# All ten tiles of the final residual addition on TensorE instead of seven, in a hybrid-attention and MoE layer

## The reference, cut to what matters

```
x   = x + gate2 * y
out = x * rsqrt(mean(x * x) + eps) * final_norm_g
```

## Time and profile before

| what | us |
|---|---|
| median of 3 runs | 1615.78 (1613.52 to 1616.71) |
| time of the profiled execution | 1616.98 |
| its span, first to last instruction | 1615.2 |
| TensorE's last matmul group starts | 1599.57 |
| VectorE's last instruction starts | 1610.77 |

### The profile page before, as it was taken

The page is one execution under the profiler, slowest core; times in us unless marked ns, Lnnn a source line. Parts: engine busy times, 40 slices in busy tenths (PEclk is TensorE's granted clock), DMA queues, the critical chain, the costliest instruction groups (busy, mean ns, idle before and its releaser), DMA issues.

```text
span 1615.2 us, 22297 instructions
## 1 busy us (share of the span) xinstructions
PE 1528.0 (95%) x8284; PEld 1275.9 (79%) x8284; DVE 973.8 (60%) x1466; ACT 665.1 (41%) x899; POOL 306.0 (19%) x231
## 2 busy tenths in 40 slices
PE   4999999999999989999999999999999699999966
PEld 3688888888888768888788887888888588888852
DVE  5388534045536477778777763334457777777737
ACT  6522221221122466666555632111221376676643
POOL 1021111122215201001100000000000155565520
PEclk9899999999999999999999999999999599999998
DMA  9236344230001010002200024425203379999966
GB/s 369 77 150 210 148 162 153 106 113 26 26 30 63 9 67 1 0 0 89 97 0 0 33 98 155 140 88 191 84 40 144 119 220 269 275 268 267 275 132 260
DMA packets 52876, 199.98 MB, mean 124 GB/s; under 512 B 8522, under 2 KB 17594, under 8 KB 41424
## 3 DMA queue, kind: packets, MB, share of 16 engines
q1 hardware_dynamic: 42576, 173.89, 29.7%
q0 software_dynamic: 10240, 25.28, 7.9%
HBM read 157.03 MB, written 45.15 MB: 125 GB/s over the span
## 4 chain that ended last, share of the span: by engine, by line
PE 41%; DVE 9%; DMA 6%; ACT 4%; issue 3%; POOL 1%; DVEq 0%; POOLq 0%; SPq 0%; ACTq 0%
PE psum L1594 7%; DMA xg<-h2d,x_row 4%; PE psum L1550 4%; PE psum L1695 4%; PE psum L1767 4%; PE psum L1788 4%; PE psum L1536 2%; PE psum L1533 2%; PE psum L1534 2%; PE psum L1771 2%; PE psum L1519 2%; PE psum L1704 2%; PE psum L1521 2%; PE psum L1520 2%; ACT prob L1875 2%
## 5 line engine op out<-in xcount | busy, mean ns | idle before, releaser
L352 PE MATMUL psum<-h_hi,w_hi 128*128 128x512 f32 x720 | 182.6, 362 | 2.1 <-issue 2.1
L352 PE MATMUL psum<-h_lo,w_hi 128*128 128x512 f32 x720 | 179.8, 358 | 0.0
L352 PE MATMUL psum<-h_hi,w_lo 128*128 128x512 f32 x720 | 179.4, 357 | 0.0
L2112 DVE TENSOR_TENSOR pT_lo<-psum,pT_hi 128x512 fp32r<-128x512 f32 x192 | 126.3, 686 | 55.2 <-ACT pT_hi L1881 55.2
L689 POOL TENSOR_TENSOR w_lo<-w_raw,w_hi 128x1024 fp32r<-128x1024 f32 x32 | 79.2, 2475 | 337.9 <-ACT w_hi L539 337.9
L1881 ACT CAST pT_hi<-psum 128x512 fp32r<-128x512 f32 x192 | 104.5, 588 | 84.2 <-PE psum L1550 84.0
L352 PEld LDWEIGHTS psum<-h_hi,w_hi 128*128 128x128 f32 x720 | 119.7, 188 | 23.8 <-issue 3.5
L352 PEld LDWEIGHTS psum<-h_lo,w_hi 128*128 128x128 f32 x720 | 119.5, 188 | 21.7 <-issue 0.5
L352 PEld LDWEIGHTS psum<-h_hi,w_lo 128*128 128x128 f32 x720 | 119.5, 188 | 21.2
L833 DVE SCALAR_TENSOR_TENSOR ada_junk<-adaT,cs_rows 128x1024 f32<-128x1024 f32 x64 | 85.9, 1342 | 69.5 <-DMA adaT<-in_w_adaT 66.6
L1875 ACT ACTIVATE prob<-psum,nmax,q_row 128x1536 f32<-128x1536 f32 x64 | 104.6, 1634 | 32.1 <-DVE nmax L2106 32.0
(11 more groups left out here) (374 smaller groups left out, 3056.6 us busy)
## 6 DMA issues: line engine op xcount, KB each, us to landing
gu_raw<-in_w_gu SPq DMA_DIRECT2D x32, 1024.0 KB, 5.8
w_raw<-in_w_in SPq DMA_DIRECT2D x16, 1024.0 KB, 4.8
adaT<-in_w_adaT SPq DMA_DIRECT2D x16, 1024.0 KB, 6.0
dn_raw<-in_w_dn SPq DMA_DIRECT2D x16, 1024.0 KB
gates<-gst SPq DMA_DIRECT2D x14, 640.0 KB, 3.1
y_sum<-stage SPq DMA_DIRECT2D x13, 512.0 KB, 5.0
xt<-in_x SPq DMA_DIRECT2D x10, 512.0 KB, 7.7
merged<-gates SPq DMA_DIRECT2D x8, 640.0 KB, 3.9
```

Of the source, the lines that this page charges most:

```text
L352: mm = pe.matmul(psum[:, par_sets[j] + g:par_sets[j] + g + w], a[j][:, k, :], b[:, k, g:g + w], start=(k == 0 and a is w_hi and b is h_hi) ...
L2112: nc.vector.tensor_tensor(pT_lo[b][g % 2][:], psum[:, TP + 512 * b:TP + 512 * b + 512], pT_hi[b][g % 2][:], ALU.subtract).then_inc(s[f"a_t ...
```

## The change

The list of tiles that VectorE adds is gone. TensorE forms the sum of all ten tiles in PSUM, in the order 0 to 9, with tile t in slot t modulo 4; from tile 4 on, residual t waits until VectorE has finished tile t-4. ScalarE waits for TensorE's `f_sum` for every tile. VectorE's `join`, the semaphore `f_summed` and the three calls are taken out; its order is otherwise the same.

```diff
--- before.py
+++ after.py
@@ -1245,16 +1245,14 @@
                 body()
 
         y = [at(f"y_{t}", [P, D], F32, RKV + 4 * t * KB) for t in range(TILES)]
-        BY_PE = (0, 1, 2, 3, 4, 6, 8)
-        BY_DVE = [t for t in range(TILES) if t not in BY_PE]
 
         def total(t):
 
-            return psum[:, 1024 * (BY_PE.index(t) % 4):1024 * (BY_PE.index(t) % 4) + D] if t in BY_PE else x1[:, t, :]
+            return psum[:, 1024 * (t % 4):1024 * (t % 4) + D]
 
         final_g = at("final_g", [P, D], F32, RA + 24 * KB)
         junk = [at(f"junk{j}", [P, D], F32, RA + (28 + 4 * j) * KB) for j in range(2)]
-        for n in "clear gated sum summed sq rt normed st dve_c".split():
+        for n in "clear gated sum sq rt normed st dve_c".split():
             s["f_" + n] = sem("b6_" + n)
         with nc.Block() as block:
             @block.sync
@@ -1842,9 +1840,8 @@
                 if_spare(pe, body)
 
                 def residual(t):
-                    n = BY_PE.index(t)
-                    if n >= 4:
-                        pe.wait_ge(s["f_normed"], BY_PE[n - 4] + 1)
+                    if t >= 4:
+                        pe.wait_ge(s["f_normed"], t - 3)
                     for h in (0, 512):
                         pe.matmul(total(t)[:, h:h + 512], ident[:], x1[:, t, h:h + 512], start=True, stop=False)
 
@@ -1856,12 +1853,12 @@
                 pe.wait_ge(s["e_y"], 2 * NE)
                 pe.wait_ge(s["f_clear"], 1)
                 pe.wait_ge(s["f_all"], 1)
-                for t in BY_PE[0:4]:
+                for t in range(4):
                     residual(t)
-                for n, t in enumerate(BY_PE):
+                for t in range(TILES):
                     join(t)
-                    if 3 <= n < len(BY_PE) - 1:
-                        residual(BY_PE[n + 1])
+                    if 3 <= t < TILES - 1:
+                        residual(t + 1)
 
             @block.scalar
             def _(act):
@@ -2080,10 +2077,7 @@
                 nc.scalar.activation(rt[:, 0:1], eps[:], ACT.Sqrt)
 
                 for t in range(TILES):
-                    if t in BY_PE:
-                        act.wait_ge(s["f_sum"], BY_PE.index(t) + 1)
-                    else:
-                        act.wait_ge(s["f_summed"], BY_DVE.index(t) + 1)
+                    act.wait_ge(s["f_sum"], t + 1)
                     nc.scalar.activation(junk[t % 2][:], total(t), ACT.Square, accum_out=ssq[:, t:t + 1]).then_inc(s["f_sq"], 1)
                     act.wait_ge(s["f_sq"], t + 1)
                     if t % 2:
@@ -2524,10 +2518,6 @@
                     dve.wait_ge(landed[t], Y_IN[t])
                     tt(y[t][:], y[t][:], gt2_row[int(t >= CTX_TILES)][:].rearrange("p k n -> p (k n)"), ALU.mult).then_inc(s["f_gated"], 1)
 
-                def join(t):
-                    dve.wait_ge(s["f_gated"], t + 1)
-                    tt(x1[:, t, :], x1[:, t, :], y[t][:], ALU.add).then_inc(s["f_summed"], 1)
-
                 def finish(t):
 
                     r, a, b = rstd[:, t:t + 2], nsq[:, t:t + 2], ntmp[:, t:t + 2]
@@ -2544,9 +2534,6 @@
                 for t in range(0, TILES, 2):
                     gate(t)
                     gate(t + 1)
-                    for u in (t, t + 1):
-                        if u in BY_DVE:
-                            join(u)
                     if t == 4:
                         dve.wait_ge(s["f_final"], 16)
                     if t >= 4:
```

## The result

Over eleven runs each the changed kernel takes 1619.31 us (1618.70 to 1621.11) and the kernel before 1614.38 us (1611.96 to 1617.00): ratio 1.003 with a 95% interval of 1.0021 to 1.0039, slower by 3.4 to 6.3 us. The forecast was 1619.8 us and +4.0. The medians lie 4.93 us apart.

A forecast was written before the change was run, and what follows sets the result against it. VectorE ran longest, with TensorE also near its limit. VectorE's 2.28 us freed against waits of 2.80 and 3.52 us for TensorE's added tiles gave +4.04 us, taking the median 1615.78 to 1619.8 us; range 1617.5 to 1621.9.

The forecast's parts named there:

- Part 1: VectorE's additions go: tile 5's is hidden already, those of tiles 7 and 9 free 2 x 1.14 = 2.28 us.
- Part 2: TensorE gets three tiles more, 10.3 us; twelve groups 1.72 us apart from residual 4 at 1590.34, ending at 1611.24.
- Part 3: TensorE's added waits for VectorE's PSUM slots and gates are met in advance: 0, at most 1.2 us; tightest margin 1.3 us.
- Part 4: After tile 9's y pass: square 0.04, root 1.43, reciprocal 0.11, last pair 3.26 us; VectorE ends at 1616.08.
- Part 5: Stores at the end: none added or dropped, so the last 3.16 us stay.
- The sum: End of VectorE moves from 1612.04 to 1616.08, +4.04 us; median becomes 1619.8 us, slower by 0.25%.
- Rival A: Added TensorE passes overlap, VectorE stays the bound and loses two additions: 1613.5 us, 0.14% down; chance 0.06.
- The rule from the Trainium skill: Judge TensorE's headroom by weight loads' busy share: over half its time free, three tiles hidden; the prediction held against it.
- Rival B: Mechanism holds, but an earlier clock rise in TensorE's first stretch keeps the difference under 3.2 us: about 1618.7 us; chance 0.20.
- Rival C: Clock falls back inside the tail, 2 us per 4 us at half clock: 1621.8 us or far more; chance 0.04.

The follow-up runs named there:

- the first experiment: Changed kernel, but tile 5's addition stays on VectorE while tiles 7 and 9 move to TensorE; ratio to the kernel before 0.9994 (0.9984 to 1.0005).
- the dead additions: Changed kernel with three VectorE additions put back as dead work into a buffer nothing reads; ratio to the kernel before 1.0018 (1.0006 to 1.0031).
- early residuals: First four residuals made without the wait for `f_all`, behind four idle copies; ratio to the kernel before 0.9982 in that kernel, 1.0000 in the changed one.
- late residuals: Residual passes of tiles 4 to 9, removed from the changed kernel with their PSUM slot waits kept; ratio to the kernel before 0.9992 (0.9980 to 1.0005).

## Why the prediction was right

*Part 1, the additions.* The addition of tile 5 was hidden: shown by the first experiment, where it costs nothing on VectorE and 3.44 us on TensorE. Those of tiles 7 and 9 were on the path, but mis-sized: I took 1.14 us for one from the distance of two starts, and the removal gave 1.25 to 1.28. In the kernel before, gates 6 and 7 began at 1591.39, 3.53 us ahead of the step at 1594.92; in the changed one it is 1591.88 - 1589.62 = 2.26. With it VectorE alone would have gained 2.5 instead of 2.28 us. It did not matter to the end, because TensorE sets it.

*Part 2, TensorE's twelve groups.* Predicted 20.90 us from residual 4 to the end of y 9 (1590.34 to 1611.24); measured 1588.56 to 1607.55 + 1.88, 20.87. This was the term that made the sum.

*Part 3, the waits at nothing.* Right: no group behind the first starts late. That the nearest wait was met 1.3 us in advance was right as well (tile 2's pass ended at 1592.87 + 1.28 = 1594.15, and residual 6 started at 1595.53: 1.38); the dead additions used up that margin, and only then did the residuals of tiles 6 and 8 come late.

*Part 4, the last step.* Predicted 0.04, 1.43, 0.11 and 3.26 us; measured from the end of y 9 at 1609.43: 0.10, 1.43, 0.11 and 3.27. The 0.06 us is nearly all that was off here.

*Part 5, the stores.* 1617.5 - 1614.34 = 3.16 us, as before.

*The sum.* +4.04 predicted, +4.08 in F. The medians differ by 4.93, with 3.4 to 6.3 in the interval; 0.3 us of the excess shows in this trace as a later rise of the clock, and the rest can't be told from the scatter of the tail's start. That the median of 1619.31 us lies only 0.5 us from the forecast is in part luck: the kernel before came out 1.4 us lower over eleven runs than over the three on which the forecast stood, and the difference 0.9 us larger, and the two nearly cancel. The dead additions, whose tail is within 0.3 us of the changed kernel's, measured 1.0018 in another batch, which is another sign of how wide that scatter is.

*Rival A* (VectorE stays the bound) is out: it needed some 2.0 us of TensorE per tile by the prediction, and each tile took 3.44. (Worked out again from the same rows: for tile 9's square to be in time as well, all six tiles could cost at most 2.2 us each. The finish that the prediction calls the third, of tiles 6 and 7, is the fourth.) It is true of the kernel with one tile moved. The rule from the Trainium skill (Perfetto Trace Analysis, Identifying the Most-Contended Engine) spoke for it: weight loads were busy 1.74 to 1.85 of 4 us while TensorE had no gap and held everybody up. Here the measurement decides against the weight loads' share as a sign of free time; the share of peak arithmetic, which that section names beside it, was not worked out.

*Rival B* (difference under 3.2 us by an earlier rise of the clock) did not come about: the interval is 3.4 to 6.3 us, and in the profiled executions the first sixteen records took 8.76 us in the kernel before and 8.81 to 9.98 in the others that ran them behind the wait, later and never sooner. Its mechanism is real all the same: in the pair of kernels with early residuals, where the first y passes run at the full clock, the kernel before could use only 1.25 us of TensorE's gain, since the addition of tile 5 stood in the way, and the difference in G was 2.83 us.

*Rival C* (the clock falls back) did not happen in the changed kernel, granted 1.00 to the end of its passes. It did in the kernel without late residuals, so the mechanism is real in this tail; but it needs a TensorE that idles, and the change left it none.

## What to carry to other kernels

Before moving work to another engine, lay out that engine's starts in the stage in question and extend them by what it gets: in this tail an addition of 1.25 us on VectorE became 3.44 us on TensorE in float32, and it paid for one tile and not for two or three. Work that lies in a wait (here tile 5's addition) is free where it is, and moving it only costs, as long as the wait is there: with early residuals the wait was gone and the same addition took its full 1.25 us. Where both engines are near their limit, look for time that the bound engine spends waiting at the start of the stage, and keep it busy there.

## What the hardware showed unexpectedly

The clock depended on work that computes nothing: with copies that are overwritten the y passes of four tiles took 7.13 us, without them 9.98. And halving TensorE's work per tile let the clock fall to half in the middle of the stage (0.61 and 0.54 granted after stretches with 2.05 of 4, 3.29 of 4 and 0.77 of 2 us busy), which cost 1.7 us. In another kernel here TensorE idled 2.62 us once and then 0.34 (the kernel before with early residuals) and the granted clock stayed at 1.00 until its passes ended; what tells the two cases apart was not tested.
